# Moving three half projections of a hybrid decoder kernel: one ahead of the mLSTM's last chunk, one behind it, one ahead of the final transposes

## The reference

```
h = rmsnorm(x, norm_mix)
z = h @ w_in                      # split: retention q,k,v,g | pool u | mLSTM q,k,v,o,i,f
y_ret  = retention(rq, rk, rv, rg, positions, ret_gn)     # 3 pairs of heads, rotary first
y_pool = pool_mix(pu, pool_w, pool_scale)  # trailing sums over 2,4,8,16 tokens, then a matmul
y_ml   = mlstm(mq, mk, mv, mo, mi, mf, ...)               # 8 chunks of 128 tokens, a state
                                                          # is carried, then head_norm, gate
x = x + concatenate([y_ret, y_pool, y_ml]) @ w_out
```

## Time and profile before

| what | value |
|---|---|
| median of 3 runs | 2640.84 us (2639.02 to 2641.95) |
| the profiled execution's own time | 2646.28 us |
| its span in the trace | 2644.5 us |
| TensorE busy | 2529.8 us, 96% of the span |
| VectorE busy | 1470.9 us, 56% |
| ScalarE busy | 713.6 us, 27% |
| GpSimd busy | 1286.0 us, 49% |
| mean granted TensorE clock | 0.98 |

### The profile page before, as it was taken

How to read it: one execution, slowest core, us unless ns; L and a number is a source line. 1 busy time by engine, 2 the same in 40 slices (tenths; PEclk the granted TensorE clock), 3 DMA queues, 4 the chain that set the end, 5 groups by cost and what they waited for, 6 DMA issues and landing times. The chain is left out here.

```text
span 2644.5 us, 29672 instructions
## 1 busy us (share of the span) xinstructions
PE 2529.8 (96%) x11892; PEld 2074.4 (78%) x11892; DVE 1470.9 (56%) x1794; ACT 713.6 (27%) x1091; POOL 1286.0 (49%) x739
## 2 busy tenths in 40 slices
PE   6899999999999989999988999999999999899996
PEld 5688777888888878887776887778888888788875
DVE  6977855773343442353778677477533333424546
ACT  3030213243333330124222010234333333211132
POOL 4322221458878754443433322224678787445431
PEclk9999999999999999999999999999999999999998
DMA  3221102112222251311132110121232323322111
GB/s 149 79 61 57 52 33 81 56 64 85 83 81 87 72 199 50 125 49 48 48 122 76 53 48 32 45 84 40 80 96 72 95 73 99 148 106 70 48 49 64
DMA packets 60601, 202.30 MB, mean 76 GB/s; under 512 B 8104, under 2 KB 16552, under 8 KB 56240
## 3 DMA queue, kind: packets, MB, share of 16 engines
q1 hardware_dynamic: 32544, 116.41, 14.2%
q10 hardware_dynamic: 27920, 83.99, 8.8%
HBM read 161.01 MB, written 32.54 MB: 73 GB/s over the span
## 5 line engine op out<-in xcount | busy, mean ns | idle before, releaser
L1674 POOL TENSOR_TENSOR w_hi<-w_raw,zero 128x1024 fp32r<-128x1024 f32 (+1 forms) x145 | 275.4, 1899 | 1119.1 <-PE proj L1729 1104.1
L1727 PE MATMUL proj<-h_hi,w_hi 128*128 128x512 f32 x1792 | 716.6, 400 | 54.5 <-DVE conv_raw L658 21.7
L1728 PE MATMUL proj<-h_hi,w_lo 128*128 128x512 f32 x1792 | 703.8, 393 | 0.0
L1729 PE MATMUL proj<-h_lo,w_hi 128*128 128x512 f32 x1792 | 703.5, 393 | 0.0
L1727 PEld LDWEIGHTS proj<-h_hi,w_hi 128*128 128x128 f32 x1792 | 340.7, 190 | 133.8 <-issue 56.5
L1728 PEld LDWEIGHTS proj<-h_hi,w_lo 128*128 128x128 f32 x1792 | 340.8, 190 | 72.0 <-issue 3.3
L1729 PEld LDWEIGHTS proj<-h_lo,w_hi 128*128 128x128 f32 x1792 | 340.1, 190 | 72.4
L1678 POOL TENSOR_TENSOR w_lo<-w_raw,w_hi 128x1024 fp32r<-128x1024 f32 (+1 forms) x145 | 389.2, 2684 | 11.4
L976 DVE TENSOR_TENSOR x<-x,proj 128x512 f32<-128x512 f32 x128 | 87.6, 686 | 331.8 <-PE proj L1729 331.8
L1685 POOL TENSOR_TENSOR w_lo<-w_raw,w_hi 128x512 fp32r<-128x512 f32 x120 | 183.4, 1529 | 97.4 <-ACT w_hi L1284 97.4
L1685 POOL TENSOR_TENSOR w_lo<-turns,w_hi 128x512 fp32r<-128x512 f32 x120 | 181.0, 1509 | 62.0 <-ACT w_hi L1284 62.0
(11 more groups left out here) (274 smaller groups left out, 4338.2 us busy)
## 6 DMA issues: line engine op xcount, KB each, us to landing
w_raw<-weights SPq DMA_DIRECT2D x170, 512.0 KB, 3.3
act_spill<-act ACTq DMA_DIRECT2D x44, 512.0 KB, 5.3
turns<-weights SPq DMA_DIRECT2D x40, 512.0 KB, 4.2
h_whole<-act_spill ACTq DMA_DIRECT2D x12, 1024.0 KB, 9.8
ffn_b_whole<-act_spill ACTq DMA_DIRECT2D x8, 1024.0 KB, 5.9
w_raw<-weights SPq DMA_DIRECT2D x16, 384.0 KB, 3.0
x<-x_in ACTq DMA_DIRECT2D x8, 512.0 KB, 8.2
ml_d<-rows_spill ACTq DMA_DIRECT2D x64, 64.0 KB, 3.3
```

Source lines behind the costliest of these rows:

```text
L1674: g.tensor_tensor(whi[:, slot, 0:n], w, zero1[:, 0:1].to_broadcast([P, n]), ALU.add).then_inc(w_hi_made, 1)
L1727: pe.matmul(out, wh, rhi, start=first, stop=False)
L1728: pe.matmul(out, wl, rhi, start=False, stop=False)
L1729: return pe.matmul(out, wh, rlo, start=False, stop=final)
```

## The change

The list is reordered; no instruction's work, size or semaphore is different, and no instruction is added or removed. The first half of `U_RET` moves between `ml_a(7)` and `ml_b(7)`, as in the chunks before; its second half stays behind `ml_b(7)`, now ahead of `gate_funcs` and `ml_norm`. The first half of `U_RET + 1` moves ahead of `ml_fin`, and its second half ahead of `pool_sums`. `U_RET + 2` stays behind `pool_sums`.

```diff
     for n in range(NCH):
-        m.append(("ml_a", n))
-        if n < NCH - 1:
-            m.append(("half", U_MO + n + 1, 0))
-        m.append(("ml_b", n))
-        if n < NCH - 1:
-            m.append(("half", U_MO + n + 1, 1))
-    m += [("gate_funcs",), ("ml_norm",), ("unit", U_RET), ("ml_fin",), ("pool_sums",), ("unit", U_RET + 1),
-          ("unit", U_RET + 2), ("pool",)]
+        u = U_MO + n + 1 if n < NCH - 1 else U_RET
+        m += [("ml_a", n), ("half", u, 0), ("ml_b", n), ("half", u, 1)]
+    m += [("gate_funcs",), ("ml_norm",), ("half", U_RET + 1, 0), ("ml_fin",), ("half", U_RET + 1, 1),
+          ("pool_sums",), ("unit", U_RET + 2), ("pool",)]
```

## The result

The changed kernel is slower: 2652.22 us median (2650.89 to 2659.44, 6 runs) against 2641.39 us (2639.02 to 2643.93, 6 runs) of the kernel before. The ratio is 1.0046 with a 95% interval of 1.0033 to 1.0059, which is 8.7 to 15.6 us. The forecast was 2655 us.

The account below looks back on a forecast made before the run. TensorE, busy 96% of the span, was taken as the bound. The 8.0 us won at `ml_b` are swallowed by the new wait at `pool`; 7.0 us lost per layer, 14 in all: 2640.84 + 14 = 2655 us, range 2645 to 2663.

Parts of the forecast that it names:

- `ml_b`: At `ml_b` of chunk 7, the first half of `U_RET` covers the 5.0 us wait for `ml_s`; `U_RET` ends 8.0 us earlier.
- `ml_norm` meets a split, 2.3 us: In `ml_norm`, VectorE's L834 runs beside GpSimd's weight split and takes 2.3 us more than its 3.84 us.
- The upper bound: In `ml_norm`, 2.3 us for L834 meeting the split, the value chosen; L834's own rows gave 0 as lower bound.
- `ml_fin`: At `ml_fin`, TensorE waits from 1592.9 to 1593.8, then to 1595.7, and makes five groups of 0.46 us, to 1598.1.
- the clock falls in `ml_fin` already: Rival, chance 0.13: short waits in `ml_fin` lower the clock, the next half takes up to 3 us longer; 2661 us.
- Late start: Ahead of `pool_sums`, VectorE idles from 1600.3 to 1604.0 for a half to empty; `pool_sums` starts 4.5 us later, at 1604.6.
- `pool_sums` 21.0 us: VectorE's `pool_sums` meets two GpSimd splits, takes 21.0 us instead of 17.0, and ends at 1625.6 instead of 1617.07.
- The base of 13.2 us: Time of `pool_sums` on VectorE without any GpSimd split beside it: 13.2 us.
- The terms for the two splits: In `pool_sums`, time added by the two GpSimd splits it meets: 3.6 us for the first, 4.2 us for the second.
- Wait at `pool`: At `pool`, TensorE makes two products by 1616.5, then waits 9 us for the end of `pool_sums`.
- Clock behind it, 3.0 us: Behind the wait at `pool`, some 6 us at clock 0.50 cost TensorE 3.0 us more before the next projection.
- The deciding point that the prediction gave for full clock: End of `pool_sums` at which the layer comes out even: 1621.6 without the lower clock, 1618.6 with it.

Follow-up runs that it names:

- the kernel with `pool_sums` first: The changed kernel with `pool_sums` moved ahead of the second half of `U_RET + 1`, GpSimd's splits as they are: 2643.58 us, ratio 1.0005 to before.
- splits held: The changed kernel with GpSimd's splits of `U_RET + 3` and `U_RET + 4` held until `ml_norm` and `pool_sums` are done: 2630.38 us, ratio 0.9967 to before.
- second part alone: The kernel before with only the halves of `U_RET + 1` put around `ml_fin`, `U_RET` whole behind `ml_b(7)`: 2659.97 us, ratio 1.0078.

## Why the prediction was right, step by step

- **`ml_b`**: no wait, full clock, start at 1580.0 forecast and 1579.90 measured. Right.
- **`ml_norm` meets a split, 2.3 us**: measured 6.05 - 3.84 = 2.2 us, and 0 when the split is held. The upper bound, taken from L898, was right; L834's own rows, which had never met GpSimd, would have misled.
- **`ml_fin`**: waits of 0.9 and 1.4 us forecast, 0.89 and 1.22 measured. But I had the five groups at full clock, 2.3 us; they took 1599.34 - 1595.52 = 3.8 us at 0.55. The rival "the clock falls in `ml_fin` already" (chance 0.13) was true, at a price of 1.5 us, not 3. `pool_sums` so started at 1605.7, not 1604.6.
- **Late start**: forecast 3.7 us idle on VectorE, measured 4.67; the step is shown by the kernel with `pool_sums` first.
- **`pool_sums` 21.0 us**: measured 1625.8 - 1605.7 = 20.1 us. The base of 13.2 us was right to a tenth. The terms for the two splits, 3.6 and 4.2 us, were too large: the rows give (2.35 - 1.21) + (2.25 - 0.17) = 3.2 and (1.74 - 0.17) + (2.19 - 0.17) = 3.6. I had taken each GpSimd instruction at its whole length. The rows show it shorter from the end of the VectorE instruction ahead of it (`w_hi` 1618.61 - 1616.85 = 1.76 us, not 1.9), and the held copy ends with it, so that its own 0.17 us is not added on top. This error and the one in `ml_fin` cancel, which is luck: the end was forecast at 1625.6 and came at 1625.76.
- **Wait at `pool`**: 9 us forecast, 8.15 measured, for TensorE came 1.0 us later than I had it.
- **Clock behind it, 3.0 us**: from the restart to the next projection 1632.68 - 1625.82 = 6.9 us, against 4.7 at full clock: 2.1 us within the stage. The clock was 0.50 for 3.6 us and then 0.92.

Per layer 6.5 us (6.2 in the first) against 7.0; both layers 12.7 against 14; 10.8 us between the medians. The path, the late start, the two meetings and the wait were right; that the number came out so near owes something to errors of opposite sign. The three mis-sized terms are the splits (0.4 and 0.6 us too much), the clock at `pool` (0.9 too much) and, against them, the clock in `ml_fin` (1.5 too little). The deciding point that the prediction gave for full clock, `pool_sums` over at 1621.6, fits the second layer of the kernel with `pool_sums` first: its `pool_sums` ends 1611.1 - 1562.7 = 48.4 us into the stage, which is 1621.3 in the times of before, the clock stayed up behind the wait of 3.6 us, and that layer's stage came out even.

## What to carry to other kernels

A stall at one place of an in-order list says how much can be won there, not how much arrives: write down, for the engine that is about to be late instead, when each of its next results is needed and how much slack each has. An item that lets an engine with little slack wait for a fresh result of the bottleneck engine (here the emptying of one half ahead of `pool_sums`) can cost more than the stall did; put independent work of that engine ahead of it. And where GpSimd and VectorE both work on SBUF, a helper's work started by the bottleneck's progress moves with it: check what it will fall on, and hold it where it has time.

## What the runs showed of the hardware

- A GpSimd instruction holds up the smallest VectorE instruction on SBUF in full: copies of 2 to 8 columns took 1.74 to 2.25 us in place of 0.17. It holds also for three-operand instructions with two SBUF inputs: L875 took 3.02 us in place of 1.28. Those with one input in PSUM went by undisturbed: at 1605.11 L654 took 0.69 us, and `w_hi`, started 0.04 us behind it, its 1.89; the six reads of `ml_fin` took 4.03 us beside a split (before, 1595.52 to 1599.90) and 4.03 us without one (second part alone). The Trainium skill's page SBUF — State Buffer ("SBUF: two separate sides") says that whoever starts first keeps the shared ports for its whole instruction; these rows agree, in both directions: `w_hi` took 2.57 us in place of 1.89 when a VectorE addition ran first. Recorded starts a few hundredths apart don't tell who that is: L875 stands at 1605.84 and `w_hi` at 1605.88, and it was L875 that waited.
- What one split cost `pool_sums` hardly depended on what it fell on: 3.2 us (with a `w_hi` that had begun 0.6 us ahead of it) and 3.6 us in the change, 3.8 us before.
- The clock fell to 1.2 GHz after two short waits, 0.89 and 1.22 us, with 0.66 us of transposes between them (0.55 over the next 3.8 us, 1.00 over the 19 us ahead). With the waits gone (splits held), the same block ran in 3.34 us of busy time instead of 0.66 and 4.07. But the length of a wait alone doesn't decide: with `pool_sums` first, a single wait of 3.62 us was followed by 1.00 over 4.9 us. What in the two short waits and the transposes brought the clock down is not shown.
